# Memory attention of eight samples: value products in rounds of four batches instead of two

## The chip, the cores and the metric

The kernel runs on one core of one Trainium2 chip. The metric is the device time of one execution in microseconds (us); the median of three runs of the kernel before is 3339.95 us (3338.22 to 3339.97). Engines: PE is TensorE, with its weight loads shown apart as PEld; DVE is VectorE, ACT is ScalarE, POOL is GpSimd, SP is SyncE.

## The reference

One inference step of a two-layer decoder trunk for a prompt of 512 rows and for 8 samples of 4 rows each. Each layer has a half-step SwiGLU, then a token mixer (a state-space scan in layer 0, dilated window attention in layer 1) beside a memory attention of 4 heads, then a second half-step SwiGLU. The change is in the memory attention of the sample group, whose keys and values come from a cache of their own for each layer and each sample:

```python
def mem_attention(q, mem_kv):
    b, L = q.shape[:2]
    qh = q.reshape(b, L, MEM_HEADS, MEM_HD)
    s = jnp.einsum('blhd,bmhd->bhlm', qh, mem_kv[:, :, 0]).astype(jnp.float32) * (MEM_HD ** -0.5)
    p = jax.nn.softmax(s, axis=-1)
    o = jnp.einsum('bhlm,bmhd->blhd', p, mem_kv[:, :, 1].astype(jnp.float32))
    return o.reshape(b, L, MEM_Q).astype(q.dtype)
```

For the samples b is 8, L is 4, m runs over 256 memory rows, and the head width is 256 for each of 4 heads, so that the values of one sample are 256 x 1024 numbers of four bytes, one megabyte.

## The kernel before

The engines' programs are written out by hand, one block per engine, and every order and every wait (a semaphore and a count) stands in the code. Most of the program is dense products: weights come in by SP's queue, are split into a high and a low part by ACT and DVE, and PE forms three products for each piece (line 981 in `product`). Between them stands, once per layer, `attention` on PE (line 1109), with `attention_loads` on POOL (line 2115) that brings in its keys and values.

**Four buffers.** `kvr` has four buffers of one megabyte. POOL issues 18 loads into them in turn (load number idx goes to buffer idx % 4): two of the prompt's keys and values, eight with the samples' keys, and then eight with the samples' values, idx 10 to 17, one per sample. Before a buffer is loaded anew, POOL waits until PE has read it. For the first four value loads (idx 10 to 13) that is a wait on the transposes of the keys (`ks_tr`); for the last four (idx 14 to 17) it is a wait on the value products of the first four samples (`vb_done`):

```python
what, last = ... else ("vb_done", NB * l + (idx - 14) // 2 * 2 + 2)
```

So loads 14 and 15 wait until samples 0 and 1 are done, and loads 16 and 17 until samples 2 and 3 are.

**The samples' part on PE.** Keys are transposed (line 1164, `rows_of`), scores are formed four samples at a time, each in a column group of its own of 32 PE columns (line 1174), the softmax is done by DVE and ACT, the probabilities are transposed back (line 1180) and DVE copies them into `PZ` (line 1648). Then come the value products, line 1191: for each sample four matmuls (two halves t of the memory rows, two halves k of the output columns) of 128 rows by 32 columns with 512 elements each. Sample b writes PE column group b % 4. The two accumulators, banks 6 and 7, collect all eight samples: the first four start them, the last four stop them. The loop takes two samples at a time and waits for their two loads first (`land`), then raises `vb_done` by two:

```python
for b0 in range(0, NB, 2):
    land(10 + b0)
    land(11 + b0)
    for t in range(2):
        for k in range(2):
            for b in (b0, b0 + 1):
                q = b % 4 * 32
                mm = pe.matmul(PS[q:q + 32, 6 + k, :], PZ[:, t, b, :], ...)
    mm.then_inc(s["vb_done"], 2)
```

The profile lists each of these matmuls as two records, so that four samples are 32 records.

**What follows.** ACT copies both banks to `Ob` (line 728), PE transposes it (line 1195), and DVE copies it to `M` (line 1653), with which the attention is over (`att_done`). In layer 0 the output projection comes next: ACT and DVE split the 24 pieces of the mixed rows (`H` by line 901, `L` by line 1964), and PE multiplies them (line 981). In layer 1 the dilated attention comes next. Its keys and values (`kvd`, 3 MB), a table (`tab`, 1 MB) and the samples' new rows (`kvn`, 0.2 MB) are issued by POOL (lines 2228 to 2230) right behind the last value load, in the same queue, and PE's next instruction (line 1398) waits for all three. POOL then waits for `att_done` and issues the loads of the cached windows into `Kc` (lines 2241, 2243, 2239), which PE transposes at line 1447.

Of the kernel before, what the change touches and what calls it, by code (L numbers as in the profile page):

```python
# [27 lines left out]
SEQ, NB, NT = 512, 8, 4  # L28
# [130 lines left out]
def build_trunk(nc, A, O):  # L159
    with ExitStack() as ctx:  # L160
        s = {n: ctx.enter_context(nc.semaphore(n)) for n in SEMS}
# [199 lines left out]
        def by_batch(ap, *steps):  # L361

            return bass.AP(ap.tensor, ap.offset, [list(ap.ap[0])] + [list(x) for x in steps])
# [609 lines left out]
        def _(pe):  # L974
# [134 lines left out]
            def attention(l, q=None):  # L1109
                q = yT  # L1110
                land = lambda idx: pe.wait_ge(kv_in[idx % 4], 16 * (LANDED[idx % 4] * l + idx // 4 + 1))
# [18 lines left out]
                for h in range(MH):  # L1130
# [12 lines left out]
                    for k in range(2):  # L1143
                        for t in range(2):
                            mm = pe.matmul(PS[:, 2 + k, :], kvr[:, 1, t, (2 * h + k) * P:(2 * h + k + 1) * P], PT[:, t, :], start=t == 0, stop=t == 1)  # L1145
# [23 lines left out]
                for i in range(4):  # L1169
                    a, half = i // 2, i % 2  # L1170
                    pe.wait_ge(s["ks_ev"], 16 * l + 4 * i + 4)
                    for j in range(4):
                        for q in range(4):
                            mm = pe.matmul(PS[32 * q:32 * q + 32, 4, 0:NM], QZ[:, 4 * half + j, 4 * a + q, :], KT[(4 * i + q) % 6][:, j, :], start=i == 0 and j == 0, stop=i == 3 and j == 3)
# [6 lines left out]
                tr.then_inc(s["s_tr"], 1)  # L1181
                pe.wait_ge(s["pz_ready"], l + 1)
                pe.wait_ge(s["ks_ev"], 16 * l + 16)
                for b0 in range(0, NB, 2):
                    land(10 + b0)
                    land(11 + b0)
                    for t in range(2):
                        for k in range(2):
                            for b in (b0, b0 + 1):
                                q = b % 4 * 32  # L1190
                                mm = pe.matmul(PS[q:q + 32, 6 + k, :], PZ[:, t, b, :], kvr[:, (10 + b) % 4, t, k * 512:(k + 1) * 512], start=b < 4 and t == 0, stop=b >= 4 and t == 1)
                    mm.then_inc(s["vb_done"], 2)
                pe.wait_ge(s["so_ev"], l + 1)
                for hk in range(8):
                    tr = pe.transpose(PS[:, hk // 4, (hk % 4) * P:(hk % 4 + 1) * P], Ob[:, hk * P:(hk + 1) * P], ident)
# [13 lines left out]
            for l in range(DEPTH):  # L1209
                ffn(l, 0)  # L1210
                if l == 0:
# [171 lines left out]
                    dense(ph["qm", 0], hH_of, hL_of, pos=lambda j: QPOS[j])  # L1383
                    stats(KI)
                    attention(0)
                    n.t += 24
                    n.unscaled += 8
                    dense(ph["out", 0], lambda k: H24[:, k, :], lambda k: L24[:, k, :], ready=lambda k: h_ready(k, 24), summed=True)
                else:
                    folded_stats()  # L1390
                    dense(ph["in_b"], hH_of, hL_of, ready=h_ready)
                    dense(ph["qm", 1], hH_of, hL_of)
                    attention(1)

                    pe.wait_ge(s["dil_in"], 48)
# [57 lines left out]
                    for st in range(16):  # L1453
# [3 lines left out]
                        for g, c0, c1 in OLD:  # L1457
                            mm = pe.matmul(PS[:, 3 + g, 0:c1 - c0], QZD[:, 2 * g + st % 2, st // 2, :], KTb[:, st % 4, c0:c1], start=st == 0, stop=st == 15)
# [3 lines left out]
                    for g in range(GD):  # L1462
                        for kv in range(KVH):
                            mm = pe.matmul(PS[:, 6, g * NS:(g + 1) * NS], QN[:, 2 * g + kv, :], KTn[:, 2 * g + kv, :], start=kv == 0, stop=kv == 1)
# [14 lines left out]
                    for g in range(GD):  # L1479
                        mm = pe.matmul(PS[:, 2, 0:256], PTn[:, g, :], kvn[:, g * 512 + 256:(g + 1) * 512], start=False, stop=g == GD - 1)  # L1480
# [580 lines left out]
        def _(pool):  # L2061
# [53 lines left out]
            def attention_loads(l, q, norms=0):  # L2115

                order = [(None, 0), (None, 1)] + [(b, c) for c in range(2) for b in range(NB)]
                for idx, (b, c) in enumerate(order):
                    if idx >= 4:

                        what, last = ("kt_tr", l + 1) if idx == 4 else ("pv_ready", MH * (l + 1)) if idx == 5 else \
                            ("ks_tr", 16 * l + 2 * (idx - 5)) if idx < 14 else ("vb_done", NB * l + (idx - 14) // 2 * 2 + 2)
                        pool.wait_ge(s[what], last)
                    dst = kvr[:, idx % 4]
                    if b is None:
                        src = mk[l].rearrange("p t (c n) -> p t c n", c=2)[:, :, c, :]
                    elif c:
                        src = mkc[l, b][:, :, c, :]
                    else:
                        b0, half = b // 4 * 4 + b % 2 * 2, b // 2 % 2  # L2130
                        dst = dst.rearrange("p b (t n) -> p b t n", t=2)
                        src = mkc[l, b0:b0 + 2, :, :, 0, half * 512:(half + 1) * 512].rearrange("b p t n -> p b t n")
                    pool.dma_start(dst, src).then_inc(kv_in[idx % 4], 16)
                    if idx == 3:

                        pool.wait_ge(s["att_go"], l + 1)
                        if norms:

                            pool.wait_ge(s["rb_ready"], norms)
                        pool.memset(QZ[:, :, :, :], 0.0).then_inc(s["qz_zero"], 1)  # L2140
                        pool.memset(PZ[:, :, :, :], 0.0).then_inc(s["qz_zero"], 1)
                        pool.wait_ge(s["qz_zero"], 2 * l + 2)
                        for hk in range(8):
                            z = QZ[:, hk, :, :]
                            dst = bass.AP(z.tensor, z.offset + (hk // 2) * NT, [list(z.ap[0]), [144, 2], [32, 4], [1, NT]])
                            pool.tensor_copy(dst, by_batch(q[:, hk, SEQ:T], (16, 2), (NT, 4), (1, NT))).then_inc(s["q_ready"], 1)
# [67 lines left out]
            periods(pool, period)  # L2214
            pool.wait_ge(s["group_end"], NG + 1)
            attention_loads(0, yT, 4)
            n.sq += KI
            y_sums()
# [5 lines left out]

            pool.wait_ge(s["w_mm"], ph["in_b"].u0 + 2)
            attention_loads(1, yT)
            pool.wait_ge(s["ss_ready"], 8)
            pool.dma_start(kvd[:, :, :], kvs[0:SEQ, :].rearrange("(t p) c -> p t c", p=P)).then_inc(s["dil_in"], 16)
# [70 lines left out]
```

## Time and profile before

| what | value |
|---|---|
| median of three runs (lowest, highest) | 3339.95 us (3338.22, 3339.97) |
| time of the profiled execution | 3329.86 us |
| its span on the core | 3328.2 us |
| mean granted TensorE clock | 0.97 |
| PE busy | 3100.6 us (93%) |
| DVE, ACT, POOL busy | 1476.3 us (44%), 1149.0 us (35%), 260.7 us (8%) |
| instructions | 55226 |

### The profile page before, as it was taken

What the parts mean: (1) busy time and instruction counts of PE and PEld (TensorE: products, weight loads), DVE (VectorE), ACT (ScalarE), POOL (GpSimd) and SP (SyncE); (2) the same over time, 40 slices, a digit from 0 to 9 for tenths busy, and PEclk for the clock granted to TensorE, in tenths of its full rate; (3) what the DMA queues carried; (4) which work ended last, traced back from release to release, by engine and by line L of the source; (5) the groups of instructions that cost most, each with busy time, mean ns of one, the idle gap of its engine ahead of it and who ended that gap; (6) DMA issues with size and microseconds to landing.
All of it is one profiled execution on the core that took longest, in us unless ns stands there. A gap on an engine that the chain in (4) does not pass through costs nothing.

```text
span 3328.2 us, 55226 instructions
## 1 busy us (share of the span) xinstructions
PE 3100.6 (93%) x22296; PEld 2861.7 (86%) x22296; DVE 1476.3 (44%) x2112; ACT 1149.0 (35%) x1631; POOL 260.7 (8%) x364
## 2 busy tenths in 40 slices
PE   6999998999999888989999899999898689899996
PEld 5799997888878766989999789999897477899996
DVE  4544425776767433254442534442433142544423
ACT  4433323444444244233332223332313232333322
POOL 0000000122222101000000000000000111000000
PEclk9999998999999899999999999999999888999998
DMA  6433232232222315223322142332331602222331
GB/s 202 133 88 88 82 92 59 84 94 79 80 72 84 120 41 186 83 64 88 88 86 87 55 144 85 88 88 87 110 95 62 239 23 60 68 87 85 89 89 50
DMA packets 444958, 306.48 MB, mean 92 GB/s; under 512 B 12516, under 2 KB 415644, under 8 KB 444700
## 3 DMA queue, kind: packets, MB, share of 16 engines
q1 hardware_dynamic: 421780, 231.03, 23.8%
q0 software_dynamic: 19744, 69.48, 5.8%
q10 hardware_dynamic: 3328, 4.47, 0.4%
q8 instruction: 78, 1.28, 0.2%
q14 instruction: 28, 0.23, 0.0%
HBM read 282.73 MB, written 22.20 MB: 92 GB/s over the span
## 4 chain that ended last, share of the span: by engine, by line
PE 89%; DVE 7%; ACT 2%; issue 1%; DMA 1%; ACTq 0%; POOL 0%; SPq 0%; DVEq 0%; POOLq 0%
PE PS L981 59%; PE PS L1231 9%; PE PS L1050 5%; PE PS L1027 1%; DVE yT L1537 1%; PE PS L1123 1%; PE PS L1268 1%; PE PS L1289 1%; DVE rb L1522 1%; PE PS L1362 1%; PE PS L1145 1%; PE PS L1301 1%; PE PS L1164 1%; PE PS L1408 1%; DVE xT L1552 1%
## 5 line engine op out<-in xcount | busy, mean ns | idle before, releaser
L1518 DVE TENSOR_TENSOR wlo<-raw,whi 128x1024 fp32r<-128x1024 f32 (+2 forms) x401 | 488.6, 1218 | 786.5 <-ACT whi L552 776.5
L981 PE MATMUL PS<-hH,whi 128*128 128x272 f32 x3280 | 682.6, 289 | 15.6 <-DVE hL L1533 7.6
L981 PE MATMUL PS<-hH,wlo 128*128 128x272 f32 x3280 | 678.8, 288 | 0.0
L981 PE MATMUL PS<-hL,whi 128*128 128x272 f32 x3280 | 678.8, 288 | 0.0
L552 ACT ACTIVATE whi<-raw 128x1024 fp32r<-128x1024 f32 (+2 forms) x401 | 413.0, 1030 | 617.9 <-PE PS L981 552.5
L981 PEld LDWEIGHTS PS<-hH,whi 128*128 128x128 f32 x3280 | 517.2, 189 | 18.1 <-issue 16.8
L981 PEld LDWEIGHTS PS<-hL,whi 128*128 128x128 f32 x3280 | 517.8, 189 | 0.0
L981 PEld LDWEIGHTS PS<-hH,wlo 128*128 128x128 f32 x3280 | 514.5, 189 | 0.0
L981 PE MATMUL PS<-H,whi 128*128 128x272 f32 x1984 | 411.9, 289 | 5.7 <-DVE L L1964 2.5
L981 PE MATMUL PS<-H,wlo 128*128 128x272 f32 x1984 | 410.6, 288 | 0.0
L981 PE MATMUL PS<-L,whi 128*128 128x272 f32 x1984 | 410.6, 288 | 0.0
L981 PEld LDWEIGHTS PS<-H,whi 128*128 128x128 f32 x1984 | 312.6, 189 | 6.4 <-issue 5.0
L981 PEld LDWEIGHTS PS<-L,whi 128*128 128x128 f32 x1984 | 312.9, 189 | 0.0
L981 PEld LDWEIGHTS PS<-H,wlo 128*128 128x128 f32 x1984 | 311.4, 189 | 0.0
L1231 PE MATMUL PS<-hH,whi 128*128 128x272 f32 x768 | 228.8, 298 | 3.0 <-issue 3.0
L1231 PE MATMUL PS<-hL,whi 128*128 128x272 f32 x768 | 222.9, 290 | 5.0 <-issue 5.0
L1231 PE MATMUL PS<-hH,wlo 128*128 128x272 f32 x768 | 222.7, 290 | 0.0
L747 ACT ACTIVATE H<-prod 128x544 f32 x88 | 57.9, 658 | 397.9 <-DVE prod L1684 397.9
L1231 PEld LDWEIGHTS PS<-hH,whi 128*128 128x128 f32 x768 | 146.1, 190 | 20.4 <-issue 19.3
L1231 PEld LDWEIGHTS PS<-hL,whi 128*128 128x128 f32 x768 | 146.1, 190 | 5.4 <-issue 5.4
L743 ACT ACTIVATE sg<-sg 128x544 f32<-128x544 f32 x88 | 58.1, 660 | 267.6 <-DVE sg L1675 267.6
L1231 PEld LDWEIGHTS PS<-hH,wlo 128*128 128x128 f32 x768 | 145.8, 190 | 0.0
(362 smaller groups left out, 3579.4 us busy)
## 6 DMA issues: line engine op xcount, KB each, us to landing
raw<-in_w_ffn_gu SPq DMA_DIRECT2D x176, 512.0 KB, 3.7
kvr<-in_cache_mem_kv POOLq DMA_DIRECT2D x32, 1024.0 KB, 8.2
raw<-in_w_in_a SPq DMA_DIRECT2D x57, 512.0 KB, 3.7
raw<-in_w_ffn_down SPq DMA_DIRECT2D x64, 448.0 KB, 3.6
rawm<-in_w_mem_kv SPq DMA_DIRECT2D x32, 512.0 KB, 4.6
raw<-in_w_ffn_down SPq DMA_DIRECT2D x32, 512.0 KB, 3.8
raw<-in_w_out_a SPq DMA_DIRECT2D x24, 512.0 KB, 3.7
raw<-in_w_in_b SPq DMA_DIRECT2D x20, 512.0 KB, 3.6
```

The source lines that it names most:

```text
L552: act.activation(whi[:, slot, 0:nk * P], src, ACT.Copy).then_inc(s["w_hi"], 1)
L743: act.activation(sg[:, b, :], sg[:, b, :], ACT.Silu).then_inc(s["silu_done"], 1)
L747: act.activation(H24[:, bass.ds(2 * i + b, 1), :], prod[:, b:b + 1, :], ACT.Copy).then_inc(s["mid_hi"], 1)
L981: mm = pe.matmul(PS[:, bank + h, 0:HT], w[:, slot, k * P:(k + 1) * P], x[:, h * HT:(h + 1) * HT], start=first and w is whi and x is hi_k, ...
L1027: mm = pe.matmul(PS[:, 4 + h, 0:HT], ones, sq[:, h * HT:(h + 1) * HT], start=start, stop=stop)
L1050: mm = pe.matmul(PS[:, bank, :], x[:, 2 * q + kk, t0:t0 + P], w[:, (d.u0 + q) % 2, kk * 512:(kk + 1) * 512], start=q == 0 and kk == 0 and ...
L1123: mm = pe.matmul(PS[:, 4 + 2 * (h % 2) + r // 2, (r % 2) * NM:(r % 2 + 1) * NM], q[:, 2 * h + k, r * P:(r + 1) * P], KT[(2 * h + k) // 4][ ...
L1145: mm = pe.matmul(PS[:, 2 + k, :], kvr[:, 1, t, (2 * h + k) * P:(2 * h + k + 1) * P], PT[:, t, :], start=t == 0, stop=t == 1)
L1164: tr = pe.transpose(PS[:, pairs[st % 3] + j // 2, (j % 2) * 256 + t * P:(j % 2) * 256 + (t + 1) * P], kvr[:, idx % 4, st % 2, c:c + P], ident)
L1231: mm = pe.matmul(PS[:, h, 0:HT], w[:, slot, k * P:(k + 1) * P], x[:, k, h * HT:(h + 1) * HT], start=k == 0 and w is whi and x is hH, stop= ...
L1268: pe.matmul(PS[:, 2, :], selg[:, h:h + 1].to_broadcast([NH, P]), acum[:, 0:SEQ], start=True, stop=True).then_inc(s["bc_ready"], 1)
L1518: dve.tensor_tensor(wlo[:, slot, 0:nk * P], src, whi[:, slot, 0:nk * P].bitcast(F32), ALU.subtract).then_inc(s["w_lo"], 1)
```

## The change

PE takes four samples at a time: it waits for all four value loads, issues the sixteen matmuls with the four column groups in turn, and raises `vb_done` by four. On POOL the last four value loads then all wait for `vb_done` to reach four. The number of matmuls, their operands and the bytes that are loaded stay as they are.

```diff
@@ attention, PE
-                for b0 in range(0, NB, 2):
-                    land(10 + b0)
-                    land(11 + b0)
+                for b0 in range(0, NB, 4):
+                    for b in range(b0, b0 + 4):
+                        land(10 + b)
                     for t in range(2):
                         for k in range(2):
-                            for b in (b0, b0 + 1):
+                            for b in range(b0, b0 + 4):
                                 q = b % 4 * 32
                                 mm = pe.matmul(PS[q:q + 32, 6 + k, :], PZ[:, t, b, :], kvr[:, (10 + b) % 4, t, k * 512:(k + 1) * 512], start=b < 4 and t == 0, stop=b >= 4 and t == 1)
-                    mm.then_inc(s["vb_done"], 2)
+                    mm.then_inc(s["vb_done"], 4)
@@ attention_loads, POOL
-                            ("ks_tr", 16 * l + 2 * (idx - 5)) if idx < 14 else ("vb_done", NB * l + (idx - 14) // 2 * 2 + 2)
+                            ("ks_tr", 16 * l + 2 * (idx - 5)) if idx < 14 else ("vb_done", NB * l + 4)
```

The order on PE at the value products of layer 0 (those of layer 1 change in the same way); `kv_in0` to `kv_in3` tell that a value load has landed in its buffer, `pz_ready` that `PZ` is there, and x7 or x15 stands for so many more matmuls of the kind:

```order
-L1191 MATMUL PS<-kvr,PZ 32x512 [waits kv_in2,kv_in3,ks_ev,pz_ready]
-L1191 MATMUL PS<-kvr,PZ 32x512 x7
-L1191 MATMUL PS<-kvr,PZ 32x512 [waits kv_in1,kv_in0]
-L1191 MATMUL PS<-kvr,PZ 32x512 x7
-L1191 MATMUL PS<-kvr,PZ 32x512 [waits kv_in3,kv_in2]
-L1191 MATMUL PS<-kvr,PZ 32x512 x7
-L1191 MATMUL PS<-kvr,PZ 32x512 [waits kv_in1,kv_in0]
-L1191 MATMUL PS<-kvr,PZ 32x512 x7
+L1191 MATMUL PS<-kvr,PZ 32x512 [waits kv_in3,kv_in0,kv_in2,kv_in1,ks_ev,pz_ready]
+L1191 MATMUL PS<-kvr,PZ 32x512 x15
+L1191 MATMUL PS<-kvr,PZ 32x512 [waits kv_in0,kv_in1,kv_in3,kv_in2]
+L1191 MATMUL PS<-kvr,PZ 32x512 x15
```

Four rounds with a wait each have become two: the first matmul now waits for all four buffers, and so does the seventeenth.

On POOL the order is the same before and after; only the counts that the four waits on `vb_done` ask for are others. In layer 1 these rows stand behind them in POOL's queue, and wait with them:

```order
L2133 DMA kvr<-in_cache_mem_kv 128x2x1024 [waits vb_done] x4
L2228 DMA kvd<-kvs 128x4x1536 [waits ss_ready]
L2229 DMA tab<-in_c_dil 128x2080
L2230 DMA kvn<-kvs 32x1536
L2241 DMA Kc<-in_cache_win_g 128x8x256 [waits att_done]
```

Nothing moves here; the first row's first two loads now wait for a later round of PE.

## Rows read from the trace of the kernel before

**Rows 1.** The page: shares of the chain that ended last, by engine.

```profile
PE 89%; DVE 7%; ACT 2%; issue 1%; DMA 1%; ACTq 0%; POOL 0%; SPq 0%; DVEq 0%; POOLq 0%
```

**Rows 2.** Timeline, layer 0, PE: start us, length us, what [idle before, releaser].

```profile
1266.71 1.93 PE L1174 MATMUL PS<-KT,QZ 128*32 128x256 f32 x32 [1.16 <-ACT KT L724]
1270.37 0.44 PE L1180 MATMUL PS<-con,Pb 128*128 128x128 f32 x2 [1.73 <-DVE Pb L1644]
1271.39 5.59 PE L1191 MATMUL PS<-kvr,PZ 128*32 128x512 f32 x32 [0.58 <-DVE PZ L1648]
1285.05 9.15 PE L1191 MATMUL PS<-kvr,PZ 128*32 128x512 f32 x32 [8.06 <-DMA kvr<-in_cache_mem_kv]
```

**Rows 3.** Timeline, layer 0, weight loads of the value products.

```profile
1273.33 1.03 PEld L1191 LDWEIGHTS PS<-kvr,PZ 128*32 128x32 f32 x12
...
1285.87 0.22 PEld L1191 LDWEIGHTS PS<-kvr,PZ 128*32 128x32 f32 x2 [0.64 <-issue]
1286.73 0.22 PEld L1191 LDWEIGHTS PS<-kvr,PZ 128*32 128x32 f32 x2 [0.64 <-issue]
...
1290.54 0.17 PEld L1191 LDWEIGHTS PS<-kvr,PZ 128*32 128x32 f32 x4 [0.40 <-issue]
```

**Rows 4.** Timeline, layer 0, POOL: the issues of the last four value loads.

```profile
1275.33 1.42 POOL L2133 DMA_DIRECT2D kvr<-in_cache_mem_kv  x2 [8.77 <-PE PS L1191]
1277.29 1.42 POOL L2133 DMA_DIRECT2D kvr<-in_cache_mem_kv  x2 [0.54 <-PE PS L1191]
```

**Rows 5.** The chain that ended last, around the end of layer 0's attention: start, length, what.

```profile
1271.39 3.65 PE PS L1191 x22
...
1298.04 5.81 DVE L L1964 x9
...
1313.80 6.27 PE PS L981 x48
```

**Rows 6.** Windows, layer 0: stretch, us, busy PE, PEld, DVE, ACT, POOL, granted clock, DMA share, GB/s.

```profile
1269.00:1273.00 4.00, 2.05 (x10) 0.69 (x12) 1.14 (x5) 0.56 (x2) 0.00 (x0) 1.00 0.70 279
...
1277.00:1280.00 3.00, 0.00 (x0) 0.00 (x0) 0.00 (x0) 0.00 (x0) 1.42 (x2) 0.94 0.89 244
...
1285.00:1290.00 5.00, 4.95 (x12) 1.30 (x14) 0.00 (x0) 0.00 (x0) 0.00 (x0) 0.51 0.79 320
...
1294.30:1298.80 4.50, 1.09 (x8) 0.86 (x8) 1.64 (x10) 2.40 (x4) 0.00 (x0) 1.00 0.00 0
1298.80:1304.00 5.20, 5.09 (x28) 5.12 (x29) 5.20 (x9) 5.20 (x10) 0.00 (x0) 0.67 0.00 0
```

**Rows 7.** Windows, layer 1, columns as in rows 6.

```profile
2609.00:2617.50 8.50, 4.87 (x12) 1.28 (x14) 0.00 (x0) 0.00 (x0) 0.23 (x1) 0.61 1.02 413
...
2630.60:2636.00 5.40, 5.26 (x30) 5.01 (x30) 0.00 (x0) 0.00 (x0) 1.49 (x10) 0.62 1.05 404
```

**Rows 8.** The chain that ended last, layer 1, first half of the value products.

```profile
2599.03 6.68 PE PS L1191 x31
```

**Rows 9.** Timeline, layer 1, the same places as in rows 3 and 4, and what follows.

```profile
2602.03 0.17 PEld L1191 LDWEIGHTS PS<-kvr,PZ 128*32 128x32 f32 x4 [0.29 <-issue]
...
2603.09 0.71 POOL L2133 DMA_DIRECT2D kvr<-in_cache_mem_kv  x1 [8.89 <-PE PS L1191]
...
2606.01 1.42 POOL L2133 DMA_DIRECT2D kvr<-in_cache_mem_kv  x2 [0.95 <-PE PS L1191]
...
2617.53 0.29 PEld L1191 LDWEIGHTS PS<-kvr,PZ 128*32 128x32 f32 x6 [0.45 <-issue]
...
2624.63 0.93 POOL L2241 DMA_DIRECT2D Kc<-in_cache_win_g  x1 [15.40 <-DVE M L1653]
...
2630.68 4.77 PE L1398 MATMUL PS<-con,kvd 128*128 128x128 f32 x24 [7.26 <-DMA kvn<-kvs]
```

**Rows 10.** DMA issues, 2600 to 2632 us: count, KB each, median us to landing.

```profile
kvn<-kvs POOLq DMA_DIRECT2D x1, 192.0 KB, 21.8
```

**Rows 11.** Line 1447, the first use of the cached windows: count, duration, first and last start.

```profile
L1447 PE MATMUL PS<-con,Kc x64: 272/273/421, 2721.1 to 2751.9; 128*128 128x128 f32 x48, 64*128 64x64 f32 x16
```

## The prediction

> **What bounds the kernel now.** I read the page first: PE carries 89% of the chain that ended last [rows 1], so a microsecond added to a place where PE waits or works on the chain is added to the time, unless something else is late there anyway. Then I read the timeline of the value products in each layer. In layer 0 they come in two halves of 32 records, one for samples 0 to 3 and one for samples 4 to 7. Between them PE stands 8.06 us for a DMA [rows 2]. The reader should see that this wait, not PE's speed, is the size of the gap: the second half needs four megabytes that cannot be asked for before PE has read the buffers. POOL asks for the first two at 1275.33, when samples 0 and 1 are done, and for the other two at 1277.29 [rows 4]. Last I read the windows for the granted clock, because after the gap PE runs at half of it [rows 6].
>
> Two things are visible in the half-finished rounds. The first pair of samples starts at 1271.39 on two loads alone, and the second pair starts at 1273.33 [rows 2, 3]; its loads were the last to be asked for and PE takes it up while the first pair still runs, so I read 1273.33 as the landing of the fourth load. Likewise the last pair starts at 1290.54, 5.5 us after its predecessor at 1285.05 [rows 2, 3].
>
> **The change part by part.**
>
> *The first round starts later.* It now needs four loads, so it starts at 1273.33 instead of 1271.39: 1.94 us lost.
>
> *It runs four groups at once.* A pair, sixteen records two at a time, took 3.65 us in eight steps [rows 5], some 0.43 us each with a tail. Do four groups really share a step? The score products of line 1174 are 32 records over four groups with half the elements and took 1.93 us [rows 2]; eight steps of half of 0.43 are 1.72 us, with a tail 1.9. So four run at once, and four samples should also take 3.65 us. 1273.33 + 3.65 = 1276.98, and the old first half ended at 1271.39 + 5.59 = 1276.98: what packing wins is exactly what the later start loses. The Trainium skill, "TensorE: Matmul & The Clock Gate", section "Measured speedup vs the span model", reports only 2.38 times for three column groups; as an estimate from that page four would give 3.2 times, each half would be about 0.85 us longer, and the sum below would come to about 12.5 us instead of 9.9. The row of line 1174 speaks for four, so the sum goes by the row.
>
> *The clock in the first round.* Before, PE was busy 2.05 us of the four microseconds from 1269 to 1273 and kept its full clock; from 1294.3 to 1298.8 it was busy 1.09 us of 4.5, and in the stretch that follows the clock is 0.67, that is 2 x 0.33 x 5.2 = 3.4 us at half [rows 6]. Now PE has 0.44 us of work between 1268.64 (end of the score products) and 1273.33 [rows 2], less than either. So I expect the clock to fall near the restart, for a spell of about 3.4 us, part of it before the restart. A spell costs half its length in PE work. Bounds: 0 if the clock holds, 3.4 us if all eight steps take 0.86 us [rows 3]. I take 1.4, nearest to the 3.4 us spell (half is 1.7).
>
> *The reloads start later.* The old first request was at 1275.33; the new one is at 1277.29 + 1.4 = 1278.7, 3.4 us later. All four are then asked for in a row, 0.71 us each [rows 4]. Does the stream catch up? Its last request is 1277.29 + 1.4 + 2.13 = 1280.8 against 1278.0, 2.8 us later, and that is the lower bound with this clock (1.4 with the clock held). The DMA share is 0.89 already from 1277 to 1280 [rows 6], so the stream was limited by its start and I take the whole 3.4. The last landing moves from 1290.54 to 1293.9.
>
> *The second round starts cold and whole.* Before, the first pair of this half soaked up the half clock (0.51 from 1285 to 1290, so 4.9 us of it) while the last pair was still on its way, and the last pair then ran 1290.54 to 1294.20 at full clock. Now no work is there before 1293.9. Half clock lasted 4.9 us after this restart and 2 x 0.38 x 5.4 = 4.1 us after the restart at 2630.6 [rows 7]; with 4.6 us it costs 2.3, so the round takes 3.65 + 2.3 = 5.95 instead of 3.66. Bounds: 3.65 if the clock is full, 7.1 if it is half throughout. The end of the attention of layer 0 moves by 3.4 + 2.3 = **5.7 us**. Nothing takes that up: the chain goes on through DVE's 5.81 us of `L` pieces to PE's output projection at 1313.80 [rows 5], all of it behind the attention. For the same reason PE's own clock around 1300 costs nothing there: DVE sets that pace.
>
> *Layer 1.* The first half ran from 2599.03 to 2605.71 [rows 8], its second pair from 2602.03 [rows 9]. The new round starts at 2602.03 and with a full clock ends when the half did; PE idles longer than in layer 0, so again 1.4. The first reload moves from 2603.09 to 2606.01 + 1.4 = 2607.4, 4.3 us [rows 9]. What follows differs: PE next waits for `kvn`, which stands behind four megabytes of values and four more of `kvd` and `tab` in the same queue. It lands 21.8 us after its issue [rows 10] while the DMA engines are full (413 GB/s, share 1.02) [rows 7]. A stream without a gap keeps its delay, so line 1398 moves by up to 4.3 us; its own request moves by only 1.4 + 1.4 = 2.8 (two more issues of 0.71 us after the last wait, and the clock), the lower bound. I take **4.2**. The late second round is hidden under it: it ends at 2617.53 + 4.3 + 5.95 = 2627.8, and the old one's end, 2617.53 + 3.66, was followed by POOL's window loads, which wait for the end of the attention, 3.4 us later [rows 9]. So the attention is over at 2631.2 and `kvn` has landed at 2630.68 + 4.2 = 2634.9. That cover is near 4 us; without it each further microsecond would count. POOL's window loads behind the attention move from 2624.63 to 2631.2, and their first reader is at 2721.1 [rows 11], so they cost nothing.
>
> *Sum.* 5.7 + 4.2 = 9.9 us on the profiled execution's 3329.86, giving 3339.8. The median of the runs is 10.1 us above that execution; on the median the sum is **3349.9 us**, slower by 0.30%. A measurement of this kernel can tell about 0.2%, 6.7 us, from no change.
>
> **The rivals.**
>
> *The cost stays under what can be seen (chance 0.19).* The clock holds in the first round, because it falls only some time after PE stops (2.7 us after 1276.98: 0.94 over 1277 to 1280 [rows 6]). And four requests in a row let the stream catch up to its last request's 1.4 us. Layer 0 is then 1.4 + 2.1 (a 4.1 us spell in the second round) = 3.5, layer 1 is 1.4, together 4.9 us: 3344.9. It decides when the two first-round spells fall away, since 9.9 less 2 x 1.4 is 7.1, and a little catching up brings that below 6.7. Against it stands how little work PE has before the restart.
>
> *Half clock through both rounds (0.10).* The first round takes 7.05, the second 7.1: layer 0 has 1.96 + 3.4 + 3.4 = 8.8, layer 1 2.9 + 3.4 = 6.3, together 15.1: 3355. Against it: no restart here ran at half clock longer than 4.9 us.
>
> *Packing does not reach four groups (0.05).* If only two share a step, a round of four takes 3.4 us more at full clock: both layers' requests move by 1.96 + 3.4 and 2.9 + 3.4, the second round of layer 0 by 5.9, together 17.6: 3357.6. With the page's rate for three groups it is milder, 3352.5. The score products speak against both.
>
> *Faster (0.01).* The last load cannot land earlier than before, since no request is earlier; only the clock elsewhere could give several microseconds.
>
> **How the numbers follow.** The forecast itself, 7 to 13 us slower, has 0.65. Slower by over 0.2% is forecast, half clock and packing: 0.80. Within 0.2% is 0.19, faster 0.01. The range is 3343.5 to 3355: at the lower end it takes most of the first rival, at the upper it ends where half clock through both rounds does and leaves the two-group case out.
>
> **What would show it.** Line 1191 in layer 0 should start near 1273.3, with no pair ahead; POOL's four issues should stand in one row at 1277 to 1279; PE's wait for the DMA should grow from 8.06 to about 15 us; the second round should be 6 us long, half of it below full clock; line 1398 should come 4 us later. The prediction is wrong if the first round starts with two samples' work anyway, if the reloads' last landing moves by less than 1.5 us, or if the clock stays full.

## The result and the profile after

The changed kernel takes 3348.7 us (median of 20 runs, 3338.11 to 3352.76) against 3336.95 us for the kernel before (20 runs, 3325.32 to 3343.38): 11.75 us more, a ratio of 1.0035 with a 95% interval of 1.0027 to 1.0044, or 9.0 to 14.7 us. Its profiled execution took 3347.71 us, with a span of 3346.0 us and a mean granted clock of 0.964. The two profiled executions are 17.85 us apart, more than the medians; where that surplus lies is told in the last section.

The timeline of PE in layer 0 of the changed kernel, which answers to [rows 2] (start us, length us, what, idle before and its releaser):

```profile
1268.52 1.93 PE L1174 MATMUL PS<-KT,QZ 128*32 128x256 f32 x32 [1.15 <-ACT KT L724]
1272.19 0.44 PE L1180 MATMUL PS<-con,Pb 128*128 128x128 f32 x2 [1.73 <-DVE Pb L1644]
1275.62 6.48 PE L1191 MATMUL PS<-kvr,PZ 128*32 128x512 f32 x32 [3.00 <-DMA kvr<-in_cache_mem_kv]
1297.08 6.00 PE L1191 MATMUL PS<-kvr,PZ 128*32 128x512 f32 x32 [14.97 <-DMA kvr<-in_cache_mem_kv]
1304.22 1.09 PE L1195 MATMUL PS<-con,Ob 128*128 128x128 f32 x8 [1.14 <-ACT Ob L728]
```

The whole trace stood 1.81 us later when the last score products of layer 0 began (1268.52 against 1266.71), so all distances below are taken from that start. The first round begins at 7.10 instead of the 4.68 of the first pair, now behind a DMA and not behind DVE. It takes 6.48 us instead of the 3.65 of one pair. The wait between the rounds is 14.97 us instead of 8.06, and the second round takes 6.00 us. The transposes that follow come at 35.70 instead of 28.60: layer 0 loses 7.1 us. Their row in the kernel before:

```profile
1295.31 1.09 PE L1195 MATMUL PS<-con,Ob 128*128 128x128 f32 x8 [1.11 <-ACT Ob L728]
```

POOL's issues there, against [rows 4]: one row of four instead of two rows of two.

```profile
1282.44 2.85 POOL L2133 DMA_DIRECT2D kvr<-in_cache_mem_kv  x4 [14.05 <-PE PS L1191]
```

The first reload is asked for at 13.92 after that start, where it was 8.62: 5.3 us later. The last one, three issues of 0.71 us behind it, is asked for at 16.06, where it was 11.29 [rows 4]: 4.8 us later. The second round, which waits for the landing of that last load, begins at 28.56; the last pair, which waited for it before, began at 23.83 [rows 3]: 4.7 us later.

The windows that answer to [rows 6] (stretch, its us, busy time of PE, PEld, DVE, ACT and POOL, granted clock, DMA share, GB/s):

```profile
1269.00:1273.00 4.00, 1.89 (x30) 0.83 (x22) 1.28 (x5) 0.56 (x2) 0.00 (x0) 1.00 1.00 409
1273.00:1276.00 3.00, 0.38 (x4) 0.23 (x8) 0.15 (x1) 0.00 (x0) 0.00 (x0) 0.76 0.24 98
1276.00:1280.00 4.00, 4.00 (x24) 1.03 (x20) 0.00 (x0) 0.00 (x0) 0.00 (x0) 0.50 0.02 4
1280.00:1283.00 3.00, 2.11 (x16) 0.31 (x8) 0.00 (x0) 0.00 (x0) 0.56 (x1) 0.77 0.00 0
1297.00:1303.20 6.20, 6.00 (x32) 1.49 (x32) 0.00 (x0) 0.06 (x1) 0.00 (x0) 0.61 0.00 0
```

The half clock of the first round lasts 2 x (0.24 x 3 + 0.50 x 4 + 0.23 x 3) = 6.8 us, from about 1274.6, a microsecond before the round begins, to about 1281.4, shortly before it ends; the second round has half clock for 2 x 0.39 x 6.2 = 4.8 us. The DMA engines stand still from about 1276 to 1283, while PE works through what they have brought.

Layer 1, against [rows 9], PE and then POOL:

```profile
2606.75 0.44 PE L1180 MATMUL PS<-con,Pb 128*128 128x128 f32 x2 [1.73 <-DVE Pb L1644]
2609.68 5.06 PE L1191 MATMUL PS<-kvr,PZ 128*32 128x512 f32 x32 [2.49 <-DMA kvr<-in_cache_mem_kv]
2629.50 5.39 PE L1191 MATMUL PS<-kvr,PZ 128*32 128x512 f32 x32 [14.76 <-DMA kvr<-in_cache_mem_kv]
2636.03 1.09 PE L1195 MATMUL PS<-con,Ob 128*128 128x128 f32 x8 [1.14 <-ACT Ob L728]
2641.63 5.29 PE L1398 MATMUL PS<-con,kvd 128*128 128x128 f32 x24 [4.51 <-DMA kvn<-kvs]
```

```profile
2615.20 0.72 POOL L2133 DMA_DIRECT2D kvr<-in_cache_mem_kv  x1 [12.25 <-PE PS L1191]
2616.45 2.14 POOL L2133 DMA_DIRECT2D kvr<-in_cache_mem_kv  x3 [0.54 <-issue]
...
2619.87 0.52 POOL L2230 DMA_DIRECT2D kvn<-kvs  x1
2638.34 0.93 POOL L2241 DMA_DIRECT2D Kc<-in_cache_win_g  x1 [17.95 <-DVE M L1653]
```

Two rows of the kernel before that [rows 9] does not have, PE and POOL:

```profile
2598.01 0.44 PE L1180 MATMUL PS<-con,Pb 128*128 128x128 f32 x2 [1.73 <-DVE Pb L1644]
```

```profile
2608.71 0.52 POOL L2230 DMA_DIRECT2D kvn<-kvs  x1
```

Here the transposes of line 1180 serve as the common point (2606.75; 2598.01 in the trace before). The first reload is asked for 8.45 us behind it, not 5.08, so 3.4 us later; `kvn` itself 13.12 us, not 10.70, so 2.4 us later; line 1398 starts 34.88 us behind it, not 32.67, so 2.2 us later. The second round ends at 2634.89 and the attention is over when POOL goes on at 2638.34, still 3.3 us before `kvn` lets PE go on: the late round is hidden, as it was before.

Together the two places account for 7.1 + 2.2 = 9.3 us of the 11.75.

### The profile page after: what moved, and what is told of

The parts are those of the page before. It is cut to its first block, busy times and chain, and to the rows that moved or that the text cites. A ratio compares the mean times of both kernels' runs of the same rounds, so it can differ in the third digit from the quotient of the medians.

```text
span 3346.0 us, 55226 instructions
## 1 busy us (share of the span) xinstructions
PE 3104.4 (93%) x22296; PEld 2867.1 (86%) x22296; DVE 1476.3 (44%) x2112; ACT 1149.4 (34%) x1631; POOL 261.6 (8%) x364
## 4 chain that ended last, share of the span: by engine, by line
PE 89%; DVE 6%; DMA 2%; ACT 2%; issue 1%; ACTq 0%; POOL 0%; SPq 0%; DVEq 0%; POOLq 0%
PE PS L981 59%; PE PS L1231 9%; PE PS L1050 5%; PE PS L1027 2%; PE PS L1268 1%; PE PS L1289 1%; DVE yT L1537 1%; DVE rb L1522 1%; PE PS L1123 1%; PE PS L1164 1%; PE PS L1362 1%; PE PS L1145 1%; PE PS L1301 1%; DMA kvr<-in_cache_mem_kv 1%; PE PS L1408 1%
```

## The experiments

All kernels below the first row were timed against the kernel before on the same chip, 12 runs of each; the kernel before was run 17 to 35 times beside them. The ratio is the one on record with its interval and not the quotient of the two medians; they differ most in e2 (11.0 us by the ratio, 8.3 by the medians) and in e5 (-6.0 and -3.6). For each, two distances were read from the trace of its one profiled execution too: from the last score products of layer 0 to line 1195 (28.60 us in the kernel before), and from the end of those of layer 1 to the dilated attention's first transposes (34.40 us before).

| kernel | median us | before, us | ratio (95% interval) | layer 0 | layer 1 |
|---|---|---|---|---|---|
| the change | 3348.7 | 3336.95 | 1.0035 (1.0027, 1.0044) | +7.1 | +2.2 |
| e1, pairs then four | 3338.44 | 3338.15 | 1.0006 (0.9991, 1.002) | +1.0 | -0.7 |
| e2, four then pairs | 3346.45 | 3338.15 | 1.0033 (1.0019, 1.0046) | +5.0 | +5.2 |
| e7, late requests only | 3342.55 | 3337.01 | 1.002 (1.0007, 1.0033) | +1.5 | +1.0 |
| e3, filled first gap | 3343.1 | 3338.15 | 1.0016 (1.0003, 1.0029) | +4.7 | +1.0 |
| e4, both gaps, 19 | 3341.57 | 3338.15 | 1.001 (0.9994, 1.0025) | +4.1 | +1.4 |
| e8, both gaps, 22 | 3340.88 | 3335.93 | 1.0014 (1.0, 1.0027) | +2.6 | +3.7 |
| e5, early reloads, pairs | 3329.86 | 3333.42 | 0.9982 (0.9967, 0.9997) | -2.5 | -4.6 |
| e6, early reloads, fours | 3330.0 | 3333.42 | 0.999 (0.9977, 1.0004) | +1.5 | +0.6 |

**e1: pairs for samples 0 to 3, one round of four for 4 to 7.**

```diff
-                for b0 in range(0, NB, 2):
+                for b0, nb in ((0, 2), (2, 2), (4, 4)):
```

against the kernel before, with `nb` in place of the two throughout, and POOL's waits as in the kernel before.

> Samples 0 to 3 in two pairs as before, so the last four value loads are asked for as before; samples 4 to 7 in one round of four. Theory (the cost is the late request for the reloads in both layers, plus a second round that starts whole at half clock in layer 0): only the last part remains, the second round of layer 0 starts when its last load lands (about 19 us after the first round's start), takes about 6 us, and ends 2.3 us later than before; layer 1 hides it under the wait for kvn. Sum +2.3 us against the kernel before (0 to +3.5). Rival (a round of four is slower in itself, or costs the same in either half): about half of the change's 11.75 us, +6 us.

PE in layer 0 of e1:

```profile
1268.92 1.93 PE L1174 MATMUL PS<-KT,QZ 128*32 128x256 f32 x32 [1.16 <-ACT KT L724]
...
1273.61 6.47 PE L1191 MATMUL PS<-kvr,PZ 128*32 128x512 f32 x32 [0.58 <-DVE PZ L1648]
1292.18 5.25 PE L1191 MATMUL PS<-kvr,PZ 128*32 128x512 f32 x32 [12.10 <-DMA kvr<-in_cache_mem_kv]
1298.57 1.09 PE L1195 MATMUL PS<-con,Ob 128*128 128x128 f32 x8 [1.14 <-ACT Ob L728]
```

The ratio is worth +2.0 us (-3 to +6.7). The expectation of +2.3 lies in that, but so does no change and, barely, the rival's +6. The trace, one execution, speaks against the rival in both layers (+1.0 and -0.7). The round of four took 5.25 us where the last pair took 3.66, 1.6 us more; its last load landed 0.57 us earlier than in the trace before (23.26 us behind the start of the score products against 23.83), though it was asked for 0.9 us later, so that the layer shows +1.0; single landings scatter by that much. So by the trace the second half's form is not where the change lost most of its time; the times alone would leave that open.

**e2: one round of four for samples 0 to 3, pairs for 4 to 7**, the counterpart (`((0, 4), (4, 2), (6, 2))`), POOL's waits as in the change.

> Samples 0 to 3 in one round of four, all four reloads asked for after it; samples 4 to 7 in two pairs. Theory: the late request remains in both layers, the first pair of the second half takes up the half clock while the last pair's loads are on their way. Layer 0 +4.7 us, layer 1 +2.2 to +4.2 us, together +7 to +9 us against the kernel before. Rival (the whole second round carries the cost): +2 to +4 us.

```profile
1267.18 1.93 PE L1174 MATMUL PS<-KT,QZ 128*32 128x256 f32 x32 [1.16 <-ACT KT L724]
...
1273.99 6.49 PE L1191 MATMUL PS<-kvr,PZ 128*32 128x512 f32 x32 [2.70 <-DMA kvr<-in_cache_mem_kv]
1290.57 5.03 PE L1191 MATMUL PS<-kvr,PZ 128*32 128x512 f32 x16 [10.09 <-DMA kvr<-in_cache_mem_kv]
1296.06 3.63 PE L1191 MATMUL PS<-kvr,PZ 128*32 128x512 f32 x16 [0.46 <-DMA kvr<-in_cache_mem_kv]
```

The ratio is worth +11.0 us (6.3 to 15.4); the expected +7 to +9 lies inside, the rival's +2 to +4 outside. By its point value the first half alone carries nearly the whole loss of 11.75 us; the interval would also allow little more than half of it. The last two rows show how pairs take up the half clock: the first pair runs 5.03 us in time that is spent waiting anyway, and the last pair takes 3.63.

**e7: late requests only.** PE as before, in pairs; POOL's last four value loads all wait for the fourth sample.

```diff
-... else ("vb_done", NB * l + (idx - 14) // 2 * 2 + 2)
+... else ("vb_done", NB * l + 4)
```

> Half of the change alone: pairs on PE as before, but all four reloads wait until samples 0 to 3 are done, as in the change. Theory: the first pair still starts early, so the clock holds and the first half ends as before; the requests start 2.0 us later in layer 0 and 2.9 us later in layer 1, the last landing and kvn follow them, and the second half absorbs its half clock in the first pair: +4 to +5 us against the kernel before, well under the change's 11.75. Rival (the two halves of the change cannot be told apart, all of the cost is the late request): +9 to +12 us. Second rival (the stream catches up to its last request): +1 to +2.5 us.

PE and POOL in layer 0 of e7:

```profile
1267.42 1.93 PE L1174 MATMUL PS<-KT,QZ 128*32 128x256 f32 x32 [1.15 <-ACT KT L724]
...
1287.86 8.55 PE L1191 MATMUL PS<-kvr,PZ 128*32 128x512 f32 x32 [9.86 <-DMA kvr<-in_cache_mem_kv]
1297.52 1.09 PE L1195 MATMUL PS<-con,Ob 128*128 128x128 f32 x8 [1.12 <-ACT Ob L728]
```

```profile
1278.30 2.84 POOL L2133 DMA_DIRECT2D kvr<-in_cache_mem_kv  x4 [11.02 <-PE PS L1191]
```

The ratio is worth +6.7 us (2.3 to 11.0); the expected +4 to +5 is inside, the first rival reaches into the interval at its upper end, the second (+1 to +2.5) touches its lower end. In the trace layer 0 loses only 1.5 us where its first request came 2.26 us later (1278.30 against 1275.33, with score products 0.71 us later), so there the stream made up part of it. Its last request came 1.7 us later, which is near the 1.5. In layer 1 `kvn`'s own request came 1.2 us later (11.90 us behind the transposes of line 1180, not 10.70) and line 1398 1.0 us later. The trace is thus with the second rival, whose stream catches up to its last request; the time does not settle the size. What the trace does show is that waiting with the requests, without a late and cold first round, is the smaller part of the loss in layer 0: 1.5 of 7.1 us.

**e3: idle matmuls in the first gap.** The changed kernel, with three matmuls of 128 rows by 384 columns of constants into an unread PSUM bank ahead of the wait; they add work and change no output.

```diff
-                for b0 in range(0, NB, 4):
+                for b0, fill in ((0, 3), (4, 0)):
+                    for _ in range(fill):
+                        pe.matmul(PS[:, 2, 0:3 * P], ident, con[:, 0:3 * P], start=True, stop=True)
                     for b in range(b0, b0 + 4):
                         land(10 + b)
```

> The changed kernel with three idle matmuls (128x384, into a bank that nothing reads then) on PE after PZ is there and before the wait for the four loads, 1.9 us of work at full clock in a gap of 2.4 to 3.0 us, in both layers. Theory: the clock holds, the first round takes 3.65 us instead of 6.5 and 5.1, everything behind it comes 1.4 to 2.8 us earlier in each layer: 3 to 5 us less than the changed kernel, that is +7 to +9 us against the kernel before. Rival (the clock there has nothing to do with the cost): as the changed kernel, +11.75 us.

PE in layer 0 of e3, the fill in its own row (the kernel's lines stand two lower there):

```profile
1265.89 1.93 PE L1174 MATMUL PS<-KT,QZ 128*32 128x256 f32 x32 [1.15 <-ACT KT L724]
...
1270.58 2.20 PE L1186 MATMUL PS<-con 128*128 128x384 f32 x6 [0.58 <-DVE PZ L1650]
1274.24 3.64 PE L1193 MATMUL PS<-kvr,PZ 128*32 128x512 f32 x32 [1.46 <-DMA kvr<-in_cache_mem_kv]
1292.82 5.26 PE L1193 MATMUL PS<-kvr,PZ 128*32 128x512 f32 x32 [14.94 <-DMA kvr<-in_cache_mem_kv]
```

The round of four takes 3.64 us, as long as a single pair [rows 5], where it took 6.48 without the fill. In layer 1 it takes 3.64 us too, where it took 5.06. That shows two things at once: four column groups do run at full rate side by side, and the missing clock was what lengthened the round. The ratio is worth +5.3 us (1.0 to 9.7) against the change's +11.75; the expected +7 to +9 lies inside, the rival's +11.75 outside, though the intervals of the two kernels still overlap (9.0 to 9.7). In this execution the fourth load landed later after the score products than in the change (8.35 us from their start to the round, against 7.10), so that the trace shows less of the gain than the round's length.

**e4 and e8: idle matmuls in both gaps**, nineteen more before the second round in e4, 22 in e8.

> As the run before it, and nineteen more such matmuls (12.2 us at full clock) in the gap of 15 us between the two rounds. Theory: the second round of layer 0 takes 3.65 us instead of 6.0 as well; layer 1 gains nothing more, it waits for kvn, or a little at line 1398, whose clock may be higher. Another 2.3 us less: +5 to +6.5 us against the kernel before; what is left is the late request alone. Rival (the stall is set by the clock, and packing would win without it): no slower than the kernel before.

> As e4_fill_both, with 22 instead of 19 idle matmuls between the rounds, 14.5 us instead of 12.5, so that only some 0.7 us without work is left before the last load lands in layer 0 (in e4_fill_both 2.7 us were left and the second round still took 5.3 us). Theory: the second round keeps its full clock and takes 3.65 us, 1.7 us less in layer 0 than in e4_fill_both: +1.5 to +4 us against the kernel before; what is left is the late request, as in e7_requests_only less its cold first pair. Rival (the round after the gap is slow for another reason than the clock): the second round again takes over 5 us.

PE between the rounds of layer 0 and the windows of the second round, first e4:

```profile
1279.25 12.52 PE L1186 MATMUL PS<-con 128*128 128x384 f32 x38
1294.46 5.34 PE L1193 MATMUL PS<-kvr,PZ 128*32 128x512 f32 x32 [2.69 <-DMA kvr<-in_cache_mem_kv]
```

```profile
1291.80:1294.40 2.60, 0.00 (x0) 0.00 (x0) 0.00 (x0) 0.00 (x0) 0.00 (x0) 1.00 0.54 221
1294.40:1299.90 5.50, 5.34 (x32) 1.59 (x32) 0.00 (x0) 0.04 (x1) 0.00 (x0) 0.69 0.00 0
```

then e8:

```profile
1281.04 14.46 PE L1186 MATMUL PS<-con 128*128 128x384 f32 x44
1295.90 3.64 PE L1193 MATMUL PS<-kvr,PZ 128*32 128x512 f32 x32 [0.41 <-DMA kvr<-in_cache_mem_kv]
```

```profile
1295.90:1299.60 3.70, 3.64 (x32) 1.10 (x32) 0.00 (x0) 0.00 (x0) 0.00 (x0) 1.00 0.00 0
```

In e4 the fill ended 2.7 us before the last load landed. The clock was still full when the round began and fell within it (0.69 over the 5.5 us), so the round took 5.34 us and the step that e4 was to remove was still there: a miss of the experiment, mended by e8. In e8 0.41 us were left, the clock stayed full and the round took 3.64 us, as the theory had it and the rival not; so it did in layer 1, where 1.71 us were left. The times agree with it less sharply: +3.3 us for e4 (-2.0 to +8.3) and +4.7 for e8 (0 to +9.0), which cannot be told from each other or from e3. Both expectations (+5 to +6.5, +1.5 to +4) lie inside their intervals, though neither point value lies inside its expected range. The rival of e4, that packing would win or at least not lose without the stall, is not excluded by the times, whose intervals reach to -2.0 and to 0; the traces of both kernels are later in both layers. What e8 keeps in layer 0 is the request that comes late even at full clock: its last request is 2.8 us later and the layer ends 2.6 later. In layer 1 `kvn`'s request is 2.4 us later and line 1398 is 3.7 later; what adds the rest is not shown.

**e5: early reloads, pairs.** The kernel before, with samples 4 and 5 loaded into the space of four key tiles (`KT`), which is free once the last scores are formed, and samples 6 and 7 into the buffers of samples 0 and 1.

```diff
+        vx = at("vx", [P, 2, 2, D], kt_at)
...
-("ks_tr", ...) if idx < 14 else ("vb_done", NB * l + (idx - 14) // 2 * 2 + 2)
+("ks_tr", ...) if idx < 14 else ("ss_ready", 4 * l + 4) if idx < 16 else ("vb_done", NB * l + 2)
```

> The kernel before (pairs), with the loads of samples 4 and 5 into the space of four key tiles, which is free when the last score products are done, so that they are asked for about 6.5 us earlier, right behind the first four; samples 6 and 7 go into the buffers of samples 0 and 1 when the first pair is done. Theory (the request for the reloads sets the end of the attention in layer 0 and of the kvn load in layer 1): the DMA engines no longer stand still between the two halves; layer 0 ends 5 to 7.5 us earlier and line 1398 of layer 1 starts 3 to 5 us earlier, together 8 to 12 us faster than the kernel before. Rival (the wait is set by something else behind the loads): within 2 us of the kernel before.

POOL's issues and PE in layer 0 of e5 (lines stand five lower there):

```profile
1271.79 1.42 POOL L2138 DMA_DIRECT2D vx<-in_cache_mem_kv  x2 [2.40 <-PE PS L1179]
1278.35 1.42 POOL L2138 DMA_DIRECT2D kvr<-in_cache_mem_kv  x2 [5.14 <-PE PS L1196]
```

```profile
1269.53 1.93 PE L1179 MATMUL PS<-KT,QZ 128*32 128x256 f32 x32 [1.16 <-ACT KT L729]
...
1274.41 5.72 PE L1196 MATMUL PS<-kvr,PZ 128*32 128x512 f32 x32 [0.58 <-DVE PZ L1653]
1283.04 5.11 PE L1196 MATMUL PS<-vx,PZ 128*32 128x512 f32 x16 [2.91 <-DMA vx<-in_cache_mem_kv]
1290.85 3.63 PE L1196 MATMUL PS<-kvr,PZ 128*32 128x512 f32 x16 [2.70 <-DMA kvr<-in_cache_mem_kv]
```

This is the one version whose interval lies wholly below the kernel before: the ratio is worth -6.0 us (-11 to -1). The two waits for a DMA shrink from 8.06 us plus the overlapped one to 2.91 and 2.70, and the trace has -2.5 us in layer 0 and -4.6 in layer 1. The rival (within 2 us) is outside by the point value, though the interval reaches to -1; the expected -8 to -12 overlaps the interval, but by the trace it was too much for layer 0, on which the last section has more.

**e6: early reloads, rounds of four.** e5 with the change's rounds, samples 6 and 7 waiting for the first round.

> The same early loads, with the rounds of four of the change; the loads of samples 6 and 7 wait for the first round. Theory: the first round still starts late and partly at half clock, so the last two requests come 3 to 5 us later than in the run before it, and the second round is whole and cold: 4 to 8 us slower than that run, that is 1 to 7 us faster than the kernel before. Rival (rounds of four lose only because all four reloads wait for them): as fast as the run before it.

The ratio is worth -3.3 us (-7.7 to +1.3), and the first round again waited 3.04 us for its fourth load and took 6.51 us. In its trace both places come later than in e5, by 4.0 us in layer 0 and 5.1 in layer 1, but the medians of the two differ by 0.14 us and their intervals overlap widely. The theory's -1 to -7 covers the point value, but the interval also holds no change, and in the trace the two places come 1.5 and 0.6 us later than in the kernel before, not earlier. So these runs settle neither whether e6 is faster than the kernel before nor whether it is slower than e5.

## Why the prediction was right

It gave 3349.9 us, slower by 9.9 on the median of three runs that it had; with 20 runs the step is 11.75 us (9.0 to 14.7), and the forecast case, 7 to 13 us slower, came true. By its steps, with distances from the traces of single executions:

- *The first round starts later, and packing wins back only that.* Shown. It waits for the fourth load (a DMA stands as its releaser where DVE stood), and at full clock a round takes 3.64 us in e3 and e8, the 3.65 of the prediction. The rate for three groups that the Trainium skill gives ("TensorE: Matmul & The Clock Gate", section "Measured speedup vs the span model") would by the prediction's estimate have made a round about 0.85 us longer than that; the 3.64 us speak against it for four groups here. The time alone would not, since the 12.5 us that the sum gives by it lie inside the interval.
- *The clock falls in the first round.* Right in kind, mis-sized in layer 0: taken as 1.4 us, it cost 6.48 - 3.65 = 2.8 us there, near the upper bound of 3.4. The half clock lasted 6.8 us where 3.4 were taken, and covered the round nearly to its end; in layer 1 it cost 5.06 - 3.65 = 1.4, as taken. e3 shows that it is the clock; why it stayed down longer in layer 0 than in layer 1 is not shown.
- *The reloads start later.* 3.4 us were forecast for the first request of layer 0 and 5.3 measured: the clock's surplus of 1.4, and 0.48 for a fourth load that landed 7.10 after the start of the score products instead of the 6.62 read from the old trace. In layer 1 3.4 us were measured for the 4.3 forecast; there the fourth load landed 1.1 us earlier (2.93 us behind the transposes of line 1180 against 4.02). The prediction carried the delay of the first request on to the last landing, and had the delay of the last request as its lower bound. The bound fits better: in layer 0 of the change the last request came 4.8 us later and the round that waits for it 4.7, and over the six kernels that ask for all four loads in a row (the change, e2, e3, e4, e7, e8) that start moved as far as the last request to within 0.1 us on average (0.6 at most) and 0.5 us less than the first. The sign that was given, one row of issues at 1277 to 1279, did not agree with the sum's own 1278.7; on the scale of the old trace the row stood at 1280.6 to 1283.5. e2's point value puts nearly everything on the first half, and e7's trace shows that the late request without the late round is its smaller part.
- *The second round starts cold and whole.* 5.95 us forecast, 6.00 measured in layer 0. Its half clock lasted 4.8 us, 4.6 were taken, and e8 makes it vanish.
- *Layer 1 keeps the stream's delay, and hides the second round.* The cover held: 3.3 us of the four were left. The shift was over-stated: 4.2 us forecast, 2.2 in the trace. The first request moved by 3.4 only, and the line did not keep even that: `kvn`'s own request moved by 2.4, and 21.8 us passed from that request to line 1398, 22.0 before. So here, too, the lower bound, the shift of `kvn`'s own request, was the one to take. Over the same six kernels line 1398 moved as far as that request on average, though up to 1.3 us off in a single execution, and 0.9 us less than the first reload.
- *Nothing else moves.* The output projection follows the attention as read; the chain has DVE's `L` pieces behind it as before, and DMA has 2% of the chain's share where it had 1% [rows 1].

The size of the clock's fall could have been read from the trace before. The prediction says that no restart there ran at half clock longer than 4.9 us; this stretch of layer 1 did, columns as in [rows 6], with PE's restart in it below:

```profile
2638.00:2645.00 7.00, 4.58 (x12) 3.21 (x12) 1.68 (x6) 1.82 (x4) 0.00 (x0) 0.51 0.06 18
```

```profile
2639.17 1.65 PE L1408 MATMUL PS<-KTd,M 128*128 128x128 f32 x6 [3.23 <-ACT KTn L916]
```

PE had been without work for 3.23 us, nearly as long as the 3.00 us before the first round of the changed kernel, and the half clock lasted 2 x 0.49 x 7.0 = 6.9 us, 5.8 of them behind the restart; that is about as long as the 6.8 us there.

The rest of the way from 9.3 us in the traces to 11.75 in the medians is within the interval, and no place in the program was found for it. In the sum of 9.9 the errors of the two layers, 1.4 us too little and 2.0 too much, nearly cancelled. That the time itself was met to 1.2 us is luck besides: the base was 3.0 us too high and the step 1.85 us too small. Of the rivals, the 4.9 us of the first, the 15.1 of half clock through both rounds and the 17.6 of two groups lie outside the interval; half clock came near in one place, the first round of layer 0, which took 6.48 of that rival's 7.05 us.

## What to carry to other kernels

Matmuls that can run side by side are worth packing only once their operands are there: a round that waits for the last of four loads starts at that load's landing and frees all four buffers at its end, so what decides is when the next loads can be asked for. Here packing won in the first round only what its late start lost, and a slow round counts because it delays those requests. Smaller rounds that began with the first operands also kept TensorE's clock up here (1.00 from 1269 to 1273 before [rows 6], 0.76 from 1273 to 1276 in the change), and let the first of them run cold in time that was waited out anyway (5.03 us, then 3.63, in e2). If PE waits for a DMA between two halves, look for space that falls free earlier and ask sooner, as e5 did with the key tiles.

## What the runs showed that was not expected

**The kernel scatters, and its clock with it.** Runs of one and the same kernel differ by 18 us and more (the kernel before: 3325.32 to 3343.38 beside the change, 3325.23 to 3346.66 beside e1 to e4), far more than three runs suggested, and the long ones have the lower mean clock: among the runs of before timed beside e5, 3323.49 us had a mean granted clock of 0.971 and 3341.59 us one of 0.963. One place where it can be seen is line 1478 in the dilated attention of layer 1, the same 64 records in both kernels (durations in ns: lowest, median, highest; first and last start in us). First the kernel before, then the changed one:

```profile
L1478 PE MATMUL PS<-Kc,QZD x64: 376/379/796, 2763.3 to 2783.7; 128*128 128x256 f32 x48, 64*128 64x256 f32 x16
```

```profile
L1478 PE MATMUL PS<-Kc,QZD x64: 376/483/796, 2774.5 to 2798.5; 128*128 128x256 f32 x48, 64*128 64x256 f32 x16
```

They take 20.4 us in one execution and 24.0 in the other. It is not tied to the change: from the start of line 1398 to the end of the span the trace before has 697.5 us and the changed one 704.4, but e5 and e7, with pairs, have 704.1 and 706.2, and e6 and e8, with rounds of four, 693.8 and 694.0. That is why a single pair of profiles, 17.85 us apart, overstates the change: 6.9 us of it lie behind that start and 1.8 ahead of layer 0's last score products, beside the 9.3 of the two places (0.2 go the other way elsewhere).

**The early stream of e5 gained less than expected.** Layer 0 came 2.5 us earlier where 5 to 7.5 were expected. One part is the request: samples 6 and 7 still wait for the first pair, so that the last load was asked for 9.53 us behind the start of the score products, where it was 11.29, only 1.8 us earlier. Another is the rate. In the kernel before the reloads moved 422 GB/s from 1283 to 1288; in e5, asked for while the earlier loads were still moving, they came at 322 GB/s, with the DMA share near one in both, and the last load ran out slowly. First the kernel before, then e5, then the end of e5's last load:

```profile
1283.00:1288.00 5.00, 2.95 (x8) 0.87 (x10) 0.00 (x0) 0.00 (x0) 0.00 (x0) 0.50 1.03 422
```

```profile
1276.00:1286.00 10.00, 7.09 (x34) 2.11 (x32) 0.00 (x0) 0.00 (x0) 1.42 (x2) 0.83 0.97 322
```

```profile
1287.00:1288.00 1.00, 1.00 (x6) 0.13 (x2) 0.00 (x0) 0.00 (x0) 0.00 (x0) 1.00 0.42 168
1288.00:1289.00 1.00, 0.15 (x2) 0.00 (x0) 0.00 (x0) 0.00 (x0) 0.00 (x0) 1.00 0.22 74
```

The 422 GB/s leave out a slow start: from 1276 to 1289.5 the reloads of the kernel before moved 312 GB/s, and e5's moved 310 from 1276 to 1288, so that asking early brought no higher rate, and, over the whole course, no lower one. Nor does an early request always go with a low rate: in e6, which asks as early for samples 4 and 5, layer 1 moved 408 GB/s from 2602 to 2608. What sets the rate was not tried.
